# Keys before queries in the base levels of a gated delta rule kernel

## What is computed

```python
qkv = jax.nn.silu(centred_conv(h @ w_in, conv_w))      # 5 taps along the tokens
q, k = l2_norm(q) * HEAD_DIM ** -0.5, l2_norm(k)
lmat = where(strict, (k * beta) @ k.T * decay, 0)       # per chunk of tokens
sol = triangular_solve(lmat + I, [v * beta, k * beta * exp(gc)])
# then a scan over the chunks with the state s, in both directions
o = qg @ s + (q @ k.T * decay) @ v_new
y = rms_norm(o) * silu(z) @ w_out
```

## Time and profile before

| what | us |
| --- | --- |
| median of 3 runs | 2881.23 (2880.4 to 2884.49) |
| profiled execution, its own time | 2878.12 |
| its span | 2876.3 |
| PE busy | 2650.1 (92% of the span) |
| ACT busy | 1233.4 (43%) |
| DVE busy | 1219.5 (42%) |
| POOL busy | 1287.2 (45%) |

### The profile page before, as it was taken

The page is one execution under the profiler, slowest core; times in us unless marked ns, Lnnn a source line. Parts: engine busy times, 40 slices in busy tenths (PEclk is TensorE's granted clock), DMA queues, the critical chain, the costliest instruction groups (busy, mean ns, idle before and its releaser), DMA issues.

```text
span 2876.3 us, 58157 instructions
## 1 busy us (share of the span) xinstructions
PE 2650.1 (92%) x24892; PEld 2223.1 (77%) x24892; DVE 1219.5 (42%) x2427; ACT 1233.4 (43%) x2210; POOL 1287.2 (45%) x780
## 2 busy tenths in 40 slices
PE   4699999999999665999999999999999999997898
PEld 0277777777778454888888888888888888886897
DVE  0212222222310322565565555655655566554323
ACT  2422333333322324465456545654565456443333
POOL 2032333333245524544554555455545554551353
PEclk8899999999999877999999999999999999998999
DMA  6835444455442202213222322232222222214554
GB/s 277 330 108 185 186 174 174 183 190 190 161 176 88 73 30 91 74 61 104 89 76 67 104 82 82 68 101 85 78 71 97 89 74 75 97 53 147 183 184 132
DMA packets 98897, 351.54 MB, mean 122 GB/s; under 512 B 10833, under 2 KB 15313, under 8 KB 96210
## 3 DMA queue, kind: packets, MB, share of 16 engines
q1 hardware_dynamic: 98642, 347.82, 34.3%
HBM read 335.59 MB, written 12.19 MB: 121 GB/s over the span
## 4 chain that ended last, share of the span: by engine, by line
PE 72%; POOL 12%; issue 6%; DVE 3%; DMA 3%; ACT 3%; SPq 0%; POOLq 0%; ACTq 0%; DVEq 0%
PE bank L522 8%; PE bank L524 7%; PE bank L523 7%; PE bank L684 4%; PE bank L686 4%; PE bank L685 4%; POOL wl L385 3%; PE bank L790 3%; PE bank L498 3%; POOL scratch L2059 2%; DMA raw<-w_ada 2%; PE bank L724 2%; PE bank L808 2%; PE bank L726 2%; PE bank L725 2%
## 5 line engine op out<-in xcount | busy, mean ns | idle before, releaser
L385 POOL TENSOR_TENSOR wl<-raw,wh 128x1024 fp32r<-128x1024 f32 x210 | 500.3, 2386 | 722.3 <-ACT wh L380 722.3
L380 ACT ACTIVATE wh<-raw 128x1024 fp32r<-128x1024 f32 x226 | 238.7, 1059 | 548.5 <-PE bank L686 258.4
L684 PE MATMUL bank<-hh,wh 128*128 128x512 f32 (+1 forms) x1040 | 410.6, 395 | 49.7 <-POOL wl L385 24.8
L686 PE MATMUL bank<-hh,wl 128*128 128x512 f32 (+1 forms) x1040 | 387.4, 372 | 0.9 <-issue 0.9
L685 PE MATMUL bank<-hl,wh 128*128 128x512 f32 (+1 forms) x1040 | 385.8, 371 | 1.3 <-issue 1.3
L684 PEld LDWEIGHTS bank<-hh,wh 128*128 128x128 f32 x1040 | 201.7, 194 | 86.1 <-POOL wl L385 25.9
L522 PE MATMUL bank<-hh,wh 128*128 128x512 f32 x640 | 256.8, 401 | 11.8 <-POOL wl L328 11.8
L328 POOL TENSOR_TENSOR wl<-raw,wh 128x1024 fp32r<-128x1024 f32 x56 | 136.7, 2446 | 254.7 <-ACT wh L323 254.7
L524 PE MATMUL bank<-hh,wl 128*128 128x512 f32 x640 | 250.4, 391 | 0.0
L523 PE MATMUL bank<-hl,wh 128*128 128x512 f32 x640 | 250.2, 391 | 0.0
L686 PEld LDWEIGHTS bank<-hh,wl 128*128 128x128 f32 x1040 | 201.3, 194 | 35.9 <-issue 1.7
(11 more groups left out here) (277 smaller groups left out, 5995.6 us busy)
## 6 DMA issues: line engine op xcount, KB each, us to landing
raw<-w_in SPq DMA_DIRECT2D x258, 512.0 KB, 3.5
raw<-w_ada SPq DMA_DIRECT2D x124, 512.0 KB, 6.5
raw<-w_out SPq DMA_DIRECT2D x84, 512.0 KB, 3.8
scratch<-w_ada SPq DMA_DIRECT2D x68, 512.0 KB, 6.3
scratch<-keep_g SPq DMA_DIRECT2D x16, 1024.0 KB, 6.0
scratch<-w_in SPq DMA_DIRECT2D x24, 512.0 KB, 7.0
scratch<-xT SPq DMA_DIRECT2D x2, 4096.0 KB, 12.8
keep_y<-scratch SPq DMA_DIRECT2D x30, 256.0 KB, 2.4
```

Source lines behind the costliest of these rows:

```text
L380: eng.activation(buffers(s)[0], raw[:, s % RAW, :], ACT.Copy).then_inc(sem("rear_hi"), 1)
L385: eng.tensor_tensor(buffers(s)[1], raw[:, s % RAW, :], buffers(s)[0].bitcast(F32), ALU.subtract)\
L684: pe.matmul(ps, w[:, k * P:(k + 1) * P], hhv[:, kk, t0:t1], start=first and k == k0, stop=False)
L686: done = pe.matmul(ps, r[:, k * P:(k + 1) * P], hhv[:, kk, t0:t1], start=False, stop=last and k == k1 - 1)
```

## The change

In iterations 0 to 14 the projections between the base levels trade places. The slots of every head now hold the keys first and the queries second. PE projects two quarters of the keys between base levels 0 and 1, one between 1 and 2, one between 2 and 3; then two quarters of the queries between 3 and 4 and two after 4. Keys go to bank 4 and queries to PA. DVE convolves the queries where it convolved the keys (after `level_z` 5), and the keys in two parts: two taps between `gate` and `turn_level` 4, three taps between `y_low` and `turn_inverse`. ACT's two silus trade places. Waits follow: `turn_k` also waits for the queries' convolution, `level_d` for the keys'. The list of ACT's weight copies stays as it is. Product counts and bytes are the same.

```diff
         def k_at(h):
-            return kqv_at(h) + (2 if h else 0)
+            return kqv_at(h)
         def q_at(h):
-            return kqv_at(h) + (0 if h else 2)
+            return kqv_at(h) + 2
...
             def turn_k(h):
                 pe.wait_ge(sem("k_silu"), h + 1)
+                if h:
+                    pe.wait_ge(sem("q_conv"), h + 1)
...
-                            pe.wait_ge(sem("q_conv"), i + 2)
+                            pe.wait_ge(sem("k_conv"), i + 2)
...
                 base(i, 0)
                 if more:
-                    q_quarter(n, 0, pb[4])
-                    q_quarter(n, 1, pb[4])
+                    k_quarter(n, 0, pb[4])
                     turn_v(i, 0)
-                    q_quarter(n, 2, pb[4])
-                    q_quarter(n, 3, pb[4])
-                    pe.wait_ge(sem("kq_read"), n)
+                    k_quarter(n, 1, pb[4])
                     pe.wait_ge(sem("v_conv"), 2 * n)
...
                 base(i, 1)
                 turn_v(i, 1)
                 if more:
-                    k_quarter(n, 0, PA)
+                    k_quarter(n, 2, pb[4])
...
                 base(i, 2)
                 if more:
-                    k_quarter(n, 1, PA)
+                    k_quarter(n, 3, pb[4])
...
                 base(i, 3)
                 if i:
                     turn_y(i - 1)
                 if more:
-                    k_quarter(n, 2, PA)
+                    pe.wait_ge(sem("kq_read"), n)
+                    q_quarter(n, 0, PA)
+                    q_quarter(n, 1, PA)
...
                 base(i, 4)
                 if more:
-                    k_quarter(n, 3, PA)
+                    q_quarter(n, 2, PA)
+                    q_quarter(n, 3, PA)
...
                 if more:
                     rear_split_hi(act, base + 5)
+                    silu_k(n)
+                evict(i, 5)
+                if more:
                     silu_q(n)
-                evict(i, 5)
-                if more:
-                    silu_k(n)
                     keys(n)
...
-            def conv_k(h, bank):
-                dve.wait_ge(sem("rear_done"), k_at(h) + 2)
-                for j in range(5):
+            def conv_k(h, bank, j0=0, j1=5):
+                if j0 == 0:
+                    dve.wait_ge(sem("rear_done"), k_at(h) + 2)
+                    if h:
+                        dve.wait_ge(sem("dv_turned"), 2 * h - 1)
+                for j in range(j0, j1):
                     last = conv_tap(acc[0], bank[:, :], h, 0, T, j)
-                last.then_inc(sem("k_conv"), 1)
+                if j1 == 5:
+                    last.then_inc(sem("k_conv"), 1)
...
                 turn_level(i, 2)
                 if i:
                     root_argument(i - 1)
-                if more:
-                    conv_q(n, pb[4])
                 tokens_v(i, 1)
                 turn_level(i, 3)
                 if i:
                     gate(i - 1)
+                if more:
+                    conv_k(n, pb[4], 0, 2)
                 turn_level(i, 4)
                 if i:
                     y_low(i - 1, yl, yh)
+                if more:
+                    conv_k(n, pb[4], 2, 5)
                 turn_inverse(i)
                 level_z(i, 5)
                 if more:
-                    conv_k(n, PA)
+                    conv_q(n, PA)
...
-    kqv = [h1[[h if h else KH, KH + h if h else 0, 2 * KH + 2 * h, 2 * KH + 2 * h + 1]].reshape(8, P, HALF * P) for h in range(KH)]
+    kqv = [h1[[KH + h, h, 2 * KH + 2 * h, 2 * KH + 2 * h + 1]].reshape(8, P, HALF * P) for h in range(KH)]
```

More of the change, by code:

```diff
@@ L1443, in _ @@
                     rear_split_hi(act, base + 5)
-                    silu_q(n)
+                    silu_k(n)
                 evict(i, 5)
                 if more:
-                    silu_k(n)
+                    silu_q(n)
                     keys(n)
```

## The result

The changed kernel takes 3073.4 us (median of 4 runs, 3068.7 to 3077.5), the kernel before 2882.1 us (four runs, one more than in the table of the time before): a ratio of 1.0663, 95% interval 1.0642 to 1.0684. The forecast was slower, 3024.8 us, with a range up to 3068. The time lies 5 us beyond the range; the slowing is 191 us where 144 were forecast.

What follows compares the result with a forecast made beforehand. PE was taken as the bound, 2.27 us idle per iteration. 7.0 + 2.33 = 9.3, plus 0.6 for clock, 9.9 us for 14 iterations, plus 5 for the first, gave 143.6 us and 3024.8 us; range 2984 to 3068.

Steps and rivals of the forecast that it cites:

- The bound and the room: PE bounds the kernel with 2.27 us idle per iteration; ACT's chain has no room before level 3 or level_w.
- Step 1, the order of the slots: ACT's weight copy of slot base + 3 waits for PE's second keys half, delaying base level 3 by 7.0 us.
- Step 2, the three taps: Three DVE taps between y_low and turn_inverse delay the spread, casts and level_w's second chunk by another 2.33 us per iteration.
- The clock after the first stop: Half speed for 3.4 us after PE idles ahead of base level 3 costs nothing, hidden before level_w by 2.3 us.
- Level 4 stays at +7.0: Between base levels 3 and 4 ACT's chain stays 5.38 us, so level 4 comes no later than level 3's +7.0.
- The clock after the second stop: Half speed after PE's 1 to 2.6 us idle at level_w costs 0 to 1.7 us, taken as 0.6.
- Iteration 0: Without output_root and y_low the added time is 4.1 us, taken as 5 with something for the clock.
- Iteration 15 and what follows: Iteration 15 projects nothing, so it was claimed untouched, with no added time.
- the dearer clock: Rival: both half-speed stretches paid, 2.7 and 1.7 us on 9.3, 13.7 per iteration, 3080 us in all; chance 0.06.
- The signs: Expected: ACT's L380 idle 6 to 7 us, PE about 7 and 1 to 3, clock near 0.9, iterations 105.5 to 107.5.

Runs made afterwards that it cites:

- the run with the filled stop: Changed kernel plus 28 useless 128x512 products on PE ahead of base level 3 in iterations 1 to 14: 3040.7 us. Same in the kernel before with added wait: 2990.5 us.

## Why the prediction was off

**The bound and the room.** Right. PE was the bound with 2.27 us of idle time, ACT's chain had no room ahead of levels 3 and 4 or of level_w, and both added waits were paid in full.

**Step 1, the order of the slots.** Right in mechanism, place and size. ACT's second L380 idles 6.95 us for PE's L686 and level 3 comes 7.0 us later. The kernel before with one added wait reproduces it, and moving that copy takes it away.

**Step 2, the three taps.** Right in size: 2.31 us of taps, and in iterations 1 to 14 some 34 us of waits at level_w where 33 were forecast.

**The clock after the first stop.** This is the step that failed: "After the first stop PE is not the bound: it reaches level_w some 2.3 us before the spread ends and can be slower by that much for nothing." The half speed came as the rows of before said, but it was not for nothing. The prediction let y_high and the spread move with ACT's chain at +7.0 and said nothing of the wait of ACT's copy of slot base + 4, which stands ahead of them. That copy waits for PE's second quarter of queries, which stands just ahead of level 4. With PE at full speed the wait is met (the run with the filled stop). With PE 2 us late the copy waits, and ACT's and DVE's chain to level_w is late with PE instead of hiding it: 2.0 us in each of 14 iterations, 28 us, and some 4 more since it was 3.9 us in iterations 7 and 11. With it fell "Level 4 stays at +7.0": it came at +9.0, as base level 3 alone went from 1.99 to 3.64 us. The run with y_high ahead of that copy shows the link: iteration 7 lasts 105.8 us there, +9.4 and so near the 9.3 of the two stops, though PE comes to level 4 at +9.8. The runs with filled stops show that the 2 us are the clock.

**The clock after the second stop** was sized at 0.6 us of a possible 1.7. In settled iterations it cost up to 1.5 (from +11.2 at level_w to +12.7 at the end), and about 4 more in iteration 12: some 20 us for 8.

**Iteration 0** cost 6.3 us for 5. **Iteration 15 and what follows** were called untouched, and took 6.5 us more (300.5 for 294.0 us from the first base level of iteration 15 to the end). Iteration 15 itself has 5.9 of them: 88.2 us at a granted clock of 0.77 for 82.3 at 0.83. The same work took 294.6 to 301.9 us in the experiments, without a relation to what was changed in them, and with more half speed where it was long. What decides that stays open.

**The terms together.** Stops: 135 forecast, 140 measured. Clock: 9 forecast, some 51 left, the tail's 6.5 included; the parts named above come to 55 and more. They are counted from settled iterations of 96.35 us, and iterations 1 to 14 of the kernel before hold 7 us more than fourteen of these, 3.3 of them in iteration 14, which had half speed of its own. The rival that was named for this, the dearer clock, came to 3080 us and had 0.06. It came nearest, and with the right reason, that both stretches are paid. Its sizes were too large (2.7 and 1.7 us for 2.0 and up to 1.5), and it had nothing for iteration 15, so that its total is nearer than its terms. The range ended short of it, though no row showed the hiding on which the forecast relied.

The Trainium skill's rule that stood beside it ("TensorE: Matmul & The Clock Gate", section "HAM oscillation — how this bites in real kernels") was the better guide: in this trace half speed came in every iteration from 0 to 14, and in the changed kernel it was paid.

**The signs.** The waits came as described (6.95 us on ACT, 7.15 and 1.38 + 1.06 us on PE). The iterations, at 109.1 to 109.7 us in most cases, were longer than the 105.5 to 107.5 named, one of them passed the 110 us that were to count as a failure (iteration 12, 114.8), and the granted clock of an iteration was 0.95 where 0.9 was named. The final time was missed by only 5 us beyond the range because the two stops, the larger part, were right; the term for the clock was a fifth of what it should have been.

## What to carry to other kernels

When a change reorders what one engine does, look at every instruction on the other engines that refills a buffer of it, and at what its wait now waits for: here an unchanged list on ACT turned one weight copy into a gate ahead of what PE needed next. When PE then idles for microseconds, charge half speed for the first microseconds of its work as well, and before calling that hidden, see whether the chain that is to hide it itself waits for PE. A copy that may wait belongs behind the copies that the bound engine is waiting for.

## What the runs showed of the hardware

A stop in two pieces of 0.7 to 1.5 and 1.0 to 1.3 us, with four small products between them, was followed by 10 to 17 us of half speed in nine iterations of one kernel and by none in three others of it, one of them with 1.46 and 1.05 us. A single stop of 7.15 us was followed by 3 to 8 us of half speed after work resumed. The length of the stop alone doesn't tell the price; what does stays open. A base level of 128 products of 32x32 by 32x64 took 1.99 us at a granted clock of 1.00 and 3.64 us at half speed. Useless products in the stop made two kernels faster, by 33 and 14 us.
